# The scores of linear-attention heads 1 and 3 inside the first unit of the next projection slice

## The reference

```
proj = h @ w_in                                     # nine column groups
b = jnp.cumsum(log_a, axis=3)                       # per chunk of 64 tokens
scores = jnp.einsum('bhncd,bhnsd->bhncs', q * jnp.exp(b - b_mid), k * jnp.exp(b_mid - b))
scores = jnp.where(mask, scores, 0.0)
o_intra = jnp.einsum('bhncs,bhnse->bhnce', scores, v)
...
o = o_intra + o_inter                               # forward and backward scans are summed
```

## Time and profile before

| | us |
|---|---|
| median of 3 runs | 1568.44 |
| lowest and highest | 1567.40, 1568.79 |
| the profiled execution | 1568.05 |
| its span, first to last instruction | 1566.2 |
| PE busy | 1507.3 |
| DVE busy | 1254.2 |
| ACT busy | 1065.0 |
| POOL busy | 133.2 |

### The profile page before, as it was taken

One profiled execution on the slowest core, in us unless ns is written; L12 is line 12 of the kernel. 1 busy time (PEld: TensorE's weight loads), 2 busy tenths in 40 slices (PEclk: granted clock), 3 DMA queues, 4 the chain that ended last, 5 costly groups with the idle time before them and its releaser, 6 DMA issues.

```text
span 1566.2 us, 18377 instructions
## 1 busy us (share of the span) xinstructions
PE 1507.3 (96%) x7228; PEld 1098.9 (70%) x7228; DVE 1254.2 (80%) x1144; ACT 1065.0 (68%) x1133; POOL 133.2 (9%) x97
## 2 busy tenths in 40 slices
PE   6998999999949999999999999999999999999997
PEld 5787777677837777777777777777777777777774
DVE  5359588785588898888889888888988888898885
ACT  7434335675447877777777777787787777777774
POOL 1024131000000102000000000000000101000000
PEclk9999999999969999999999999999999999999999
DMA  7111001401749999999999999999999999999991
GB/s 242 55 54 54 20 35 55 150 28 55 269 177 359 380 382 365 391 374 392 369 378 383 360 394 377 392 364 381 387 370 394 359 393 366 384 384 369 391 365 59
DMA packets 192070, 448.49 MB, mean 286 GB/s; under 512 B 12977, under 2 KB 13297, under 8 KB 191985
## 3 DMA queue, kind: packets, MB, share of 16 engines
q1 hardware_dynamic: 187440, 433.03, 74.9%
q0 software_dynamic: 3968, 12.65, 3.6%
q10 hardware_dynamic: 576, 1.64, 0.3%
HBM read 434.71 MB, written 12.58 MB: 286 GB/s over the span
## 4 chain that ended last, share of the span: by engine, by line
PE 90%; DVE 6%; issue 2%; ACT 1%; DMA 1%; POOL 0%; POOLq 0%; DVEq 0%; ACTq 0%
PE ps L904 23%; PE ps L902 23%; PE ps L903 23%; PE ps L583 5%; PE ps L585 4%; PE ps L584 4%; PE ps L937 1%; PE ps L798 1%; PE ps L832 1%; DVE slice_low L1335 1%; DVE t L1436 1%; DVE states L1421 1%; PE ps L895 1%; PE ps L854 1%; PE ps L818 1%
## 5 line engine op out<-in xcount | busy, mean ns | idle before, releaser
L1743 DVE TENSOR_TENSOR wl<-raw,wh 128x2048 fp32r<-128x2048 f32 x384 | 875.1, 2292 | 142.6 <-ACT wh L1270 137.4
L1270 ACT CAST wh<-raw 128x2048 fp32r<-128x2048 f32 x384 | 730.7, 1912 | 134.9 <-PE ps L904 133.1
L902 PE MATMUL ps<-wh,XTh 128*96 128x512 f32 x1024 | 407.9, 398 | 0.6 <-DVE XTl L1748 0.6
L904 PE MATMUL ps<-wl,XTh 128*96 128x512 f32 x1024 | 405.5, 396 | 0.0
L903 PE MATMUL ps<-wh,XTl 128*96 128x512 f32 x1024 | 402.8, 393 | 0.0
L904 PEld LDWEIGHTS ps<-wl,XTh 128*96 128x96 f32 x1024 | 165.4, 162 | 72.3
L903 PEld LDWEIGHTS ps<-wh,XTl 128*96 128x96 f32 x1024 | 166.3, 162 | 68.6
L902 PEld LDWEIGHTS ps<-wh,XTh 128*96 128x96 f32 x1024 | 165.7, 162 | 67.7 <-DVE XTl L1748 0.9
L902 PE MATMUL ps<-wh,gTh 128*96 128x512 f32 x512 | 202.0, 395 | 1.2 <-DVE gTl L1754 1.2
L904 PE MATMUL ps<-wl,gTh 128*96 128x512 f32 x512 | 201.2, 393 | 0.0
L903 PE MATMUL ps<-wh,gTl 128*96 128x512 f32 x512 | 200.8, 392 | 0.0
(11 more groups left out here) (232 smaller groups left out, 1525.6 us busy)
## 6 DMA issues: line engine op xcount, KB each, us to landing
raw<-in_w_gate SPq DMA_DIRECT2D x128, 1024.0 KB, 8.5
raw<-in_w_up SPq DMA_DIRECT2D x128, 1024.0 KB, 8.7
raw<-in_w_down SPq DMA_DIRECT2D x128, 1024.0 KB, 8.8
slice_raw<-in_w_in SPq DMA_DIRECT2D x6, 2048.0 KB, 8.0
X<-in_x_sample SPq DMA_DIRECT2D x8, 512.0 KB, 12.6
slice_raw<-in_w_out SPq DMA_DIRECT2D x2, 2048.0 KB, 9.4
X<-in_x_prompt SPq DMA_DIRECT2D x4, 512.0 KB, 5.0
h_rows<-hn SPq DMA_DIRECT2D x4, 512.0 KB, 3.3
```

The source lines that it names most:

```text
L902: pe.matmul(out, hi, rhs_h, start=first, stop=False)
L904: return pe.matmul(out, hi, rhs_l, start=False, stop=last)
L1270: act.copy(wh[:, n % CONV, :], raw[:, n % RAW, :]).then_inc(s_wh, 1)
L1743: dve.tensor_tensor(wl[:, n % CONV, :], raw[:, n % RAW, :], wh[:, n % CONV, :].bitcast(F32), ALU.subtract).then_inc(s_wl, 1)
```

## The change

In rounds whose predecessor was a rotary slice (h = 1 and h = 3), `scores(h, 0)` and `scores(h, 1)` no longer stand ahead of the unit: the unit is told to call them itself, after the waits of its sixth depth step and before that step's matmuls. Rounds 0 and 2 stay as they were. No instruction is added or taken away, and the other engines' lists are the same.

```
-            def unit(kind, s, t):
+            def unit(kind, s, t, inside=None):
...
                     for k in range(KD):
                         if t == 0:
                             slice_ready(s, k)
+                        if inside is not None and k == 5:
+                            scores(inside, 0)
+                            scores(inside, 1)
                         mm = three(bank(b), HTh[:, k, t * P:(t + 1) * P], HTl[:, t, k, :],
                                    wih[:, k, :], slice_low[s % 2][:, k, :], k)
...
                 h, t = i // NT, i % NT
-                if t == 0:
+                crowded = t == 0 and rotary(i - 1) is not None
+                if t == 0 and not crowded:
                     scores(h, 0)
                     scores(h, 1)
                 if i < BODY - 2:
-                    unit("tok" if rotary(i) is None else "dqk", FIRST + h, t)
+                    unit("tok" if rotary(i) is None else "dqk", FIRST + h, t, h if crowded else None)
```

## The result

| | before | changed |
|---|---|---|
| median, us | 1568.09 (6 runs) | 1574.03 (6 runs) |
| lowest and highest, us | 1567.23, 1568.79 | 1573.60, 1574.81 |
| span of the profiled execution, us | 1566.2 | 1571.8 |
| PE busy, us | 1507.3 | 1508.6 |

The account below looks back on a forecast made before the run. PE, 90% of the span in the chain ending last, was taken as the bound. Two places at 0.84 + 2.3 = 3.14 us gave 6.3 us, from 1568.44 to 1574.7; range 1573 to 1577.4, for 8 in 10 1570.6 to 1577.4.

Parts of the forecast that it names:

- The unit's start costs nothing either way: Rounds 1 and 3: the low part holds the unit, which starts at 148.77 and 243.89 as before; cost nothing.
- The sum at full clock, 7.81 us: Unit's start to `turn_keys` at full clock: 7.81 us in place of 6.97, so 0.84 us lost a place.
- The clock, 2.3 us a place: Unit behind the longer PE gap: low clock lasts 4.6 us after restart, half lost, 2.3 us a place (1.7 to 3.45).
- my lower end of 3.4: Shortest time the low clock was taken to last once PE works again, 3.4 us, a loss of 1.7 a place.
- the 9.7 that I had named as a sign: Expected in the changed kernel's trace: `turn_keys` 9.7 to 11 us behind the unit's start.
- What hangs behind: DVE's masks, which read the scores: DVE may wait some 0.4 us for each group, `turn_keys` doesn't wait; cost nothing.
- All of it reaches the end: PE behind both places and in the experts has no gap to make up the delay; all 6.3 us taken through.
- (a): Rival: clock returns at 149.24 and 244.8 as today; 2.4 us lost in all, time 1570.8; chance 0.10.
- (b): Rival: part of the delay made up later by a PE wait, such as a weight stream; 3.1 us, 1571.5; chance 0.05.
- (c): Rival: depth steps fill PE's gap, the unit starting at about 144.3; about 7 us faster, 1561; chance 0.06.
- (d): Rival: slow clock through the whole unit makes the mask the end, masks at 159.0; adds nothing; no chance given.

Follow-up runs that it names:

- e4: The kernel before with 11 unread matmuls put ahead of the scores in each of the two PE gaps; 1568.06 us against 1568.30 before.
- e3: The changed kernel with 24 unread matmuls put into each of the two PE gaps ahead of the unit; 1569.50 us against 1568.30 before.
- e6: The changed kernel with the scores behind seven depth steps in place of five; 1574.28 us against 1568.71 before.
- e1: The change in round 1 alone, round 3 keeping the order of the kernel before; 1571.17 us against 1568.30 before.
- e2: The change in round 3 alone, round 1 keeping the order of the kernel before; 1571.45 us against 1568.30 before.
- e9: The changed kernel with e7's DVE order and POOL's inter-chunk query product moved behind the round's last half swap; 1564.96 us against 1568.43 before.
- e5: The changed kernel with the scores behind one depth step in place of five; 1573.86 us against 1568.71 before.
- e7: The changed kernel with DVE issuing six low parts ahead of the score factors at both places; 1568.68 us against 1568.71 before.

## Why the prediction was right, point by point

Forecast: 1574.7 us, 6.3 us lost in two places. Measured: 1574.03, 5.9 us above before.

- **The unit's start costs nothing either way.** Right: 148.76 for 148.77, and 0.82 us behind the low parts' start as before. That the low part, and not the factor, was the last thing is shown by the changed kernel itself, whose unit no longer waits for the factor and starts no earlier, and by e4 (1.31 us of idle time behind fast scores).
- **The sum at full clock, 7.81 us.** e3 measured 7.77 and 7.78; the extra is 0.80 us a place for the forecast 0.84. That it fits so closely is in part luck. I had put the rope turn at its length in the trace, 0.60 us, where what counts is the distance to `turn_keys`, 0.43; and unit and scores together took 7.34 us (148.93 to 156.27) in place of 7.21, since matmuls on both sides of the scores start farther apart. The two errors nearly cancel. That the wait for the mask takes up a part of the scores' 1.6 us was right: no trace with the scores inside has a wait of `turn_keys` for the mask.
- **The clock, 2.3 us a place.** The mechanism was right (e3), the size was the mis-sized term: 9.19 - 7.77 = 1.4 us in round 1 and 10.02 - 7.77 = 2.2 us in round 3, 3.7 us in all for 4.6. The term rests on how long the low level lasts once PE works again. I took 4.6 us from four restarts; it was about 3 and 4.7 in this trace, and the first is below my lower end of 3.4, as 9.19 us is below the 9.7 that I had named as a sign. What I had not asked is when the clock had fallen: in this trace the time behind the restart is what was left of a stretch that began in the gap, 3.8 us ahead of the restart in round 1 and 2.0 us in round 3. That one place fell below my range and the other near its middle was chance. The term also counts from a kernel before that pays nothing for the clock, which its trace bears out and other executions do not (last section).
- **What hangs behind.** Right in the cost, partly wrong in the detail: DVE waited 0.60 us for the scores in round 3 and not at all in round 1, where I had 0.4 us; e6 made it 2.39 us and that cost nothing either.
- **All of it reaches the end.** Right: 5.17 us behind round 3, 5.13 at the experts' start, 5.6 at the span's end. The last 0.4 us are again clock, and no effect of the change that could be relied on: the experts began at 1.2 GHz in both traces, from 455.05 to about 459.8 before, and in the changed kernel from 460.18 to about 465.8, by the row below.

```profile
465.00:466.00 1.00, 1.00 (x4) 0.57 1.02 418
```

  In e6 it went the other way: its experts started 1.7 us later still (461.89), the low level ended at 464.9, and its span is only 0.6 us longer.

- **The rivals.** (a), the clock back when it was before, is out by the 0.50 that reaches to 151.7. (b), made up later, is out by e1, e2 and the lag that stays. (c), depth steps that fill the gap, did not happen, and for the reason given, DVE's order; e9 shows that it does once the order is another, though its gain is 3.5 us and not 7, since the scores still wait for their factors (1.19 us) and the unit could start at 144.9 and not at 144.3. (d) did not occur.

How far the two parts are settled: the split of 5.9 us into about 1.6 and 4.3 rests on two medians (e3, 1.2 us above before with an interval of -0.5 to 2.4 us; e3 by the rows of its trace 1.6), so the size of each is known to about 1 us. That both parts exist is shown.

## What to carry to other kernels

Before work is moved out of the front of a stalled block, ask what would have ended the stall without it: if that is another wait of the same length, the work was free where it stood, and it costs its full time wherever the engine has no gaps. Such a move pays only together with the producer's order, here DVE and POOL: +5.9 us alone, and -3.5 us with both, of which POOL's order gives 1.8 us even without the move. A gap that grows from 2.9 to 5.85 us has a second price on TensorE, the low clock of what runs behind it, and this (some 4 us here) was larger than what the moved work itself cost (1.6 us).

## What the runs showed of the hardware that I had not expected

- The kernel before pays for the slow clock in some executions too. In e1's trace round 3 has the old order, yet the low level came later and lasted longer: the scores took 2.02 us, PE idled 0.90 us, and then the unit ran at 0.50 from 246.36 to about 251.3, so that `turn_keys` came 8.3 us behind its start and not 7.0. The windows:

```profile
246.00:250.00 4.00, 3.64 (x9) 0.50 0.30 112
250.00:252.00 2.00, 2.00 (x8) 0.67 0.03 8
```

  Round 1 of e2, the same old order, has 7.5 us. I had read from one trace that the clock costs the old order nothing, and the prediction counts it so. Of the 33 executions of the kernel before that stand beside e1 to e4, the 16 with a mean granted clock of 0.984 or 0.985 took 1568.3 to 1570.0 us and the 17 with 0.987 or more took 1567.3 to 1568.3; all 11 of e4 have 0.987 or more. This points to a price of about 1.4 us in half of the executions. It is not shown that the two places are where it is paid, since the experts' start is slow too.
- Behind the same gap of 5.8 us the low level lasted, by the windows, 3.1 and 4.8 us after PE's restart in the changed kernel, 3.4 in e1, 3.2 in e2, 3.7 and 5.2 in e5, 5.7 and 6.2 in e6. The Trainium skill, "TensorE: Matmul & The Clock Gate", part 1, says that the release shifts against the program from run to run; these rows agree. The spread of 3.1 us is 1.5 us of time, nearly twice the change's cost at full clock in one place.
- A gap much shorter than these can be followed by the low level: in round 3 of e9 PE idled 2.04 us ahead of the unit, and the granted clock was 0.50 from 239.4 to 242.8. It cost little there, since the scores would have waited for their factors anyway (`turn_keys` came 9.36 us behind the unit's start, 9.01 in round 1).
- A DVE subtraction of 0.68 us took 2.31 us beside one POOL instruction of 2.27 us (e7). An operation that is off PE's path on a slow engine can sit in the middle of it by way of DVE.
